# The 32 late modulation tiles: one-column matmuls replaced by streams past a 32-column stationary block

## What is computed

```
mod = silu(c) @ mod_w + mod_b          # (1024) @ (1024, 6*1024), six vectors of 1024
h   = rms_norm(x) * (1 + scale1) + shift1        # vectors 0, 1
x   = x + gate1 * norm(gla_mixer(h, h_ctx))      # vector 2
h   = rms_norm(x) * (1 + scale2) + shift2        # vectors 3, 4
x   = x + gate2 * norm(swiglu(h))                # vector 5
```

## Time and profile before

| | |
|---|---|
| median of 3 runs | 1826.99 us |
| lowest, highest | 1826.46, 1835.96 us |
| span of the profiled execution | 1833.4 us |
| PE busy in it | 1770.2 us, 97% |
| PEld, DVE, ACT, POOL busy | 1468.8, 813.0, 492.5, 111.6 us |
| mean granted PE clock | 0.951 of full |

### The profile page before, as it was taken

How to read it: one execution, slowest core, us unless ns; L and a number is a source line. 1 busy time by engine, 2 the same in 40 slices (tenths; PEclk the granted TensorE clock), 3 DMA queues, 4 the chain that set the end, 5 groups by cost and what they waited for, 6 DMA issues and landing times.

```text
span 1833.4 us, 20676 instructions
## 1 busy us (share of the span) xinstructions
PE 1770.2 (97%) x8502; PEld 1468.8 (80%) x8502; DVE 813.0 (44%) x955; ACT 492.5 (27%) x508; POOL 111.6 (6%) x95
## 2 busy tenths in 40 slices
PE   8999999999889999999899999999999999999997
PEld 3889987877768888888688888887897788888885
DVE  3654123444453343343444444344545544444444
ACT  3385123112232222222322222223132222222221
POOL 0000000000200000000200000111600400000000
PEclk9999997677889999999799999999999999999998
DMA  9132232001312222233132222333221222222231
GB/s 367 58 127 70 92 141 90 0 1 46 103 57 105 92 92 96 76 96 101 47 112 92 95 111 71 95 94 141 97 88 46 85 98 93 92 92 91 83 100 72
DMA packets 29288, 169.68 MB, mean 93 GB/s; under 512 B 3376, under 2 KB 3760, under 8 KB 15536
## 3 DMA queue, kind: packets, MB, share of 16 engines
q1 hardware_dynamic: 29232, 168.88, 26.4%
HBM read 166.77 MB, written 2.10 MB: 92 GB/s over the span
## 4 chain that ended last, share of the span: by engine, by line
PE 75%; issue 20%; DVE 2%; ACT 2%; POOL 1%; DMA 0%; POOLq 0%; DVEq 0%; SPq 0%; ACTq 0%
PE bank L476 75%; POOL qd L415 1%; ACT w_hi L989 0%; POOL root L386 0%; PE bank L687 0%; DMA mod_w<-in_mod 0%; DVE y_ffn L1875 0%; DVE w_lo L1322 0%; DVE tmp L1330 0%; DVE a_lo L1596 0%; ACT L1057 0%; ACT tmp L1061 0%; DVE y_gla L1585 0%; ACT tmp L1053 0%; ACT tmp L1057 0%
## 5 line engine op out<-in xcount | busy, mean ns | idle before, releaser
L476 PE MATMUL bank<-a_hi,w_hi 128*128 128x512 f32 x1376 | 545.3, 396 | 14.4 <-DVE a_lo L1596 8.4
L476 PE MATMUL bank<-a_hi,w_lo 128*128 128x512 f32 x1376 | 539.6, 392 | 0.0
L476 PE MATMUL bank<-a_lo,w_hi 128*128 128x512 f32 x1376 | 539.4, 392 | 0.0
L1322 DVE TENSOR_TENSOR w_lo<-w_raw,w_hi 128x2048 fp32r<-128x2048 f32 x144 | 333.8, 2318 | 428.9 <-ACT w_hi L989 428.4
L989 ACT ACTIVATE w_hi<-w_raw 128x2048 fp32r<-128x2048 f32 x144 | 275.5, 1913 | 622.5 <-PE bank L476 620.2
L476 PEld LDWEIGHTS bank<-a_hi,w_hi 128*128 128x128 f32 x1376 | 260.9, 190 | 73.2 <-issue 19.4
L476 PEld LDWEIGHTS bank<-a_hi,w_lo 128*128 128x128 f32 x1376 | 260.5, 189 | 55.5
L476 PEld LDWEIGHTS bank<-a_lo,w_hi 128*128 128x128 f32 x1376 | 260.8, 190 | 54.6 <-issue 1.2
L476 PE MATMUL bank<-g_hi,w_hi 128*128 128x512 f32 x528 | 205.4, 389 | 0.0
L476 PE MATMUL bank<-g_lo,w_hi 128*128 128x512 f32 x528 | 205.4, 389 | 0.0
L476 PE MATMUL bank<-g_hi,w_lo 128*128 128x512 f32 x528 | 205.4, 389 | 0.0
(11 more groups left out here) (238 smaller groups left out, 1650.9 us busy)
## 6 DMA issues: line engine op xcount, KB each, us to landing
w_raw<-in_ffn_in SPq DMA_DIRECT2D x66, 1024.0 KB, 4.8
w_raw<-in_ffn_out SPq DMA_DIRECT2D x24, 768.0 KB, 4.2
mod_raw<-in_mod SPq DMA_DIRECT2D x32, 512.0 KB, 3.6
w_raw<-in_ffn_out SPq DMA_DIRECT2D x24, 640.0 KB, 3.9
w_raw<-in_gla_in SPq DMA_DIRECT2D x12, 1024.0 KB, 5.8
w_raw<-in_mix_in SPq DMA_DIRECT2D x10, 1024.0 KB, 4.7
mod_w<-in_mod SPq DMA_DIRECT2D x8, 1024.0 KB, 15.3
w_raw<-in_gla_out SPq DMA_DIRECT2D x4, 1024.0 KB, 5.7
```

The costliest lines, as they stand in the source:

```text
L476: return pe.matmul(out, lhs, rhs, start=first, stop=last, skip_group_check=True)
L1322: V.tensor_tensor(flat(w_lo[s]), flat(w_raw[s]), flat(w_hi[s]).bitcast(F32), ALU.subtract).then_inc(lo_done[s], 1)
```

## The change

Four tiles are taken together, as group g of 0 to 7. Silu(c) becomes the stationary operand: `sc_wide` holds, for each of the 8 chunks of channels, a block of 32 columns of which the first is silu(c) and the others are zero. The weights of four tiles stream past it as 512 columns. Chunk k and chunk k+4 write to partitions 32(k mod 4) to 32(k mod 4)+31 of bank 7, so the results are four partial rows in one bank (`mod_lines`, 8 matmuls). ACT copies the bank to `mod_line`, and four matmuls against a column of ones sum the rows and turn them into four columns in bank 7 (`mod_columns_of`). DVE adds the bias (`mod_add`). All three engines use bank 7 in turn, so `mod_lines(g)` waits for `mod_add(g-1)`.

Groups 0 to 3 stand at the end of `v_unit` 0 to 3, groups 4 to 7 at the end of the four r units; the columns of a group stand one unit later than its lines. Nothing of the late tiles is left in units 0 to 3 or behind the scan. The weights come in 16 loads of 1 MB of 8 KB a partition into two buffers that lie in x's own 16 KB, and x is loaded a second time (2 MB) when they are done. The pieces below are, in order, the new functions on PE, the end of a v unit, the r units, ACT's copy, DVE in the v and in the r units, and SP.

```diff
-            def mod_tile(j):
-
-                pe.wait_ge(mod_loaded, cnt.next(mod_loaded, 16))
-                for k in range(KD):
-                    m = mm(bank[7][:, j:j + 1], mod_raw[:, k], sc[:, k, 0:1], k == 0, k == KD - 1)
-                m.then_inc(mod_used, 1)
+            def mod_lines(g):
+
+                if g == 0:
+                    pe.wait_ge(wide_done, 2)
+                else:
+                    pe.wait_ge(mod_added, g)
+                for half in range(2):
+                    pe.wait_ge(mod_loaded[half], cnt.next(mod_loaded[half], 16))
+                    for k in range(KD // 2):
+                        m = mm(bank[7][32 * k:32 * k + 32, :], sc_wide[:, half * (KD // 2) + k],
+                               mod_raw[half][:, :, k], half == 0, half == 1)
+                    m.then_inc(mod_used, 1)
+
+            def mod_columns_of(g):
+
+                pe.wait_ge(line_copied, g + 1)
+                for j in range(4):
+                    m = mm(bank[7][:, j:j + 1], mod_line[:, j * P:(j + 1) * P], ones[:, 0:1], True, True)
+                m.then_inc(mod_mapped, 1)
...
-                mod_tile(9 + 2 * h)
+                if h:
+                    mod_columns_of(h - 1)
+                mod_lines(h)
...
             for n in range(4):
-                unit(n % 2, ((0, 1), (3, 4))[n % 2], (a_hi, a_lo), tile=16 + 2 * n)
-                mod_tile(17 + 2 * n)
-            filled[7] = True
+                unit(n % 2, ((0, 1), (3, 4))[n % 2], (a_hi, a_lo))
+                mod_columns_of(3 + n)
+                mod_lines(4 + n)
+            mod_columns_of(7)
...
+            def line_copy(g):
+                act.wait_ge(mod_used, 2 * g + 2)
+                nc.scalar.activation(mod_line[:], bank[7][:], ACT.Copy).then_inc(line_copied, 1)
...
                 split_lo(h % 2)
+                if h:
+                    mod_add(h - 1)
...
             for n in range(4):
                 split_lo(n % 2)
-
-            dve.wait_ge(mod_used, cnt.next(mod_used, 3 * KD))
-            V.tensor_tensor(mod[:, 2 * KD:5 * KD, 0], bank[7][:, 0:3 * KD], col("mod_b", 2 * KD, 3 * KD), ALU.add).then_inc(free[7], 1)
+                mod_add(3 + n)
+            mod_add(7)
...
+            sp.wait_ge(mod_used, MOD_PARTS)
+            sp.dma_start(xT[:], a["x_fm"]).then_inc(x_again, 16)
```

More of the change, by code:

```diff
@@ L60 @@
 FIRST_MODS = 4
+MOD_PARTS = 16
 LAG = 2
@@ L142, in build @@
         mod_at = top[0]
-        mod_raw = place("mod_raw", [P, KD, P])
+        mod_line = place("mod_line", [P, T])
+        sc_wide = place("sc_wide", [P, KD, 32])
+        top[0] += KB
+        x_at = top[0]
         xT = place("xT", [P, KD, T])
+        mod_raw = [place(f"mod_raw{s}", [P, 4, KD // 2, P], F32, x_at + 8 * KB * s) for s in range(2)]
         act_at = here(32 * KB)
@@ L237, in build @@
         cols_ready = sem("modulation_columns_ready")
-        mod_loaded, mod_used = sem("mod_tile_loaded"), sem("mod_tile_used")
+        mod_loaded, mod_used = [sem(f"mod_part_loaded{s}") for s in range(2)], sem("mod_part_used")
+        mod_lined, line_copied = sem("mod_line_ready"), sem("mod_line_copied")
+        mod_mapped, mod_added, wide_done = sem("mod_columns_ready"), sem("mod_columns_added"), sem("wide_condition_done")
+        x_again = sem("x_loaded_again")
         cols_loaded, x_loaded, c_loaded = sem("cols_loaded"), sem("x_loaded"), sem("context_loaded")
@@ L315, in load, with load_parts @@
                 sp.dma_start(flat(w_raw[s])[:, 0:width], src).then_inc(raw_loaded[s], 16)
[L317 to L321, removed]
+            def load_parts(q0, q1):
+                for q in range(q0, min(q1, MOD_PARTS)):
+                    g, half = q // 2, q % 2
+                    if q >= 2:
+                        sp.wait_ge(mod_used, q - 1)
+                    w = KD // 2 * P
+                    sp.dma_start(mod_raw[half][:].rearrange("p j k o -> p j (k o)"),
+                                 a["mod25"][4 * g:4 * g + 4, :, half * w:(half + 1) * w].rearrange("j p w -> p j w")).then_inc(mod_loaded[half], 16)
             for n in range(8):
@@ L332, in _, with ffn @@
             sp.dma_start(reset[:], a["reset"]).then_inc(masks_loaded, 16)
-            load_tile(0)
-            for n in range(12):
+            for n in range(4):
+                load(n % 2, a["gla_in"][n + 2])
+            load_parts(0, 2)
+            for n in range(4, 12):
                 m = n + 2
                 load(m % 2, a["gla_in"][m] if m < 12 else a["gla_out"][m - 12])
-                load_tile(2 * n + 1)
-                load_tile(2 * n + 2)
+                load_parts(2 * n - 6, 2 * n - 4)
+            sp.wait_ge(mod_used, MOD_PARTS)
+            sp.dma_start(xT[:], a["x_fm"]).then_inc(x_again, 16)
             for m in (14, 15):
                 load(m % 2, a["gla_out"][m - 12])
-            load_tile(25)
-            def ffn(w_in, w_out, tiles=()):
+            def ffn(w_in, w_out):
                 both = {x[s]: 1 for x in (hi_done, lo_done) for s in range(2)}
@@ L358, in ffn @@
                         load(j % 2, src, (k1 - k0) * UC)
-            ffn(a["ffn0_in"], a["ffn0_out"], range(26, 32))
+            ffn(a["ffn0_in"], a["ffn0_out"])
             ffn(a["ffn1_in"], a["ffn1_out"])
@@ L485, in weights, with unit @@
                 return w_hi[s][:, k, c * P:(c + 1) * P], w_lo[s][:, k, c * P:(c + 1) * P]
-            def mod_tile(j):
-                pe.wait_ge(mod_loaded, cnt.next(mod_loaded, 16))
-                for k in range(KD):
-                    m = mm(bank[7][:, j:j + 1], mod_raw[:, k], sc[:, k, 0:1], k == 0, k == KD - 1)
-                m.then_inc(mod_used, 1)
-            def unit(s, banks, acts, by_chunk=None, says=None, tile=None, roots_to=None, streamed=False):
+            def mod_lines(g):
[14 more added lines that the diff above has]
+                m.then_inc(mod_mapped, 1)
+            def unit(s, banks, acts, by_chunk=None, says=None, roots_to=None, streamed=False):
                 pe.wait_ge(lo_done[s], cnt.next(lo_done[s]))
@@ L589, in gla_unit @@
                 s = n % 2
-                unit(s, banks, (a_hi, a_lo), norm_lo if n == 0 else None, tile=2 * n)
+                unit(s, banks, (a_hi, a_lo), norm_lo if n == 0 else None)
                 if n == 0:
@@ L720, in scan @@
                     take(6)
-                    take(7)
-                    filled[6] = filled[7] = False
+                    pe.wait_ge(mod_added, MOD_PARTS // 2)
+                    filled[6] = False
                 kv(0)
@@ L759, in _ @@
             for n in range(4):
-                unit(n % 2, ((0, 1), (2, 3))[n % 2], (a_hi, a_lo), norm_lo if n == 0 else None,
-                     tile=24 + n if n else None)
+                unit(n % 2, ((0, 1), (2, 3))[n % 2], (a_hi, a_lo), norm_lo if n == 0 else None)
             def double_norm():
@@ L800, in group @@
                         pe.wait_ge(up_free, cnt.now(up_free))
-                    unit(1, (2, 3), (a_hi, a_lo), None, up_ready, roots_to=5 if first and scaled else None,
-                         tile=31 if tiles else None)
+                    unit(1, (2, 3), (a_hi, a_lo), None, up_ready, roots_to=5 if first and scaled else None)
                     cnt.expect(up_free, CPU)
@@ L1322, in split_lo, with mod_add @@
                 V.tensor_tensor(flat(w_lo[s]), flat(w_raw[s]), flat(w_hi[s]).bitcast(F32), ALU.subtract).then_inc(lo_done[s], 1)
+            def mod_add(g):
+                dve.wait_ge(mod_mapped, g + 1)
+                V.tensor_tensor(mod[:, 2 * KD + 4 * g:2 * KD + 4 * g + 4, 0], bank[7][:, 0:4], col("mod_b", 2 * KD + 4 * g, 4),
+                                ALU.add).then_inc(mod_added, 1)
             def mean_square(b, n, width):
@@ L1360, in norm_parts @@
                 lower(KD - 1)
+            V.memset(flat(sc_wide), 0.0).then_inc(wide_done, 1)
+            dve.wait_ge(wide_done, 1)
+            dve.wait_ge(silu_c_done, 1)
+            V.tensor_copy(sc_wide[:, :, 0], sc[:, :, 0]).then_inc(wide_done, 1)
             V.memset(power[:], -0.5).then_inc(const_set, 1)
@@ L1510, in _ @@
                 split_lo(n % 2)
-            dve.wait_ge(mod_used, cnt.next(mod_used, 3 * KD))
-            V.tensor_tensor(mod[:, 2 * KD:5 * KD, 0], bank[7][:, 0:3 * KD], col("mod_b", 2 * KD, 3 * KD), ALU.add).then_inc(free[7], 1)
-            cnt.expect(free[7])
-            dve.wait_ge(free[7], cnt.now(free[7]))
+                mod_add(3 + n)
+            mod_add(7)
+            dve.wait_ge(mod_added, MOD_PARTS // 2)
             V.tensor_tensor(gain[:, 2], mod[:, 2 * KD:3 * KD, 0], col("norm_g", KD, KD), ALU.mult)
+            V.tensor_tensor(gain[:, 4], mod[:, 5 * KD:, 0], col("norm_g", 3 * KD, KD), ALU.mult)
             V.scalar_tensor_tensor(gain[:, 3], mod[:, 4 * KD:5 * KD, 0], 1.0, col("norm_g", 2 * KD, KD), ALU.add, ALU.mult).then_inc(dve_step, 1)
@@ L1696, in ffn @@
                 group(0, True)
[L1697 to L1703, removed]
                 for j in range(2):
```

18 lines of the change are left out of this document (4 added, 14 removed).

## The result

| | median, us | lowest to highest | runs | profiled execution: span, mean granted clock |
|---|---|---|---|---|
| before | 1829.91 | 1826.46 to 1835.96 | 4 | 1833.4, 0.951 |
| changed | 1859.16 | 1855.94 to 1859.96 | 4 | 1858.0 (of 1859.8 us), 0.938 |

The changed kernel takes 1.0148 times as long, with a 95% interval of 1.0124 to 1.0172. It is slower by 29 us, where 26.7 were forecast.

A forecast was written before the change was run, and what follows sets the result against it. PE, busy 97% of the span, was taken as the bound. Added 52.1 us (lines 15.6, last columns 1.6, pauses 34.9) less gains of 42.6, plus 17.2 for lower clock, made +26.7 on 1826.99: 1853.7 us, range 1833 to 1884.

The forecast's parts named there:

- units 0 to 3: Removing tiles 0 to 7 there gains 6.5 us instead of 13.6, as ACT's gate chain then becomes the bound.
- v and r units, and the scan's start: Added lines, last columns, pauses and lower clock, less 27.2 us for 16 tiles and 2.1 us for a wait.
- behind it: Behind the scan, removing tiles 25, 26, 27 and 31 gains 6.8 us; tiles 24, 28, 29 and 30 count nothing.
- The gain of the tiles: Late tiles taken off PE: 6.5 us in units 0 to 3, 27.2 in v and r units, 6.8 for four others.
- The lines: Four column strips overlap fully on PE: 1.95 us a group of 8 matmuls, 15.6 us for eight groups.
- The pauses: PE waits at unit ends for the add behind DVE's split: 3 x 4.7 + 4 x 5.2 = 34.9 us, seven columns included.
- The clock: PE's granted clock falls to half after all seven pauses, costing 17.2 us; bounds 0 and 22 us.
- wait for DVE's add: At the scan's start PE's wait for the one bias add, queued behind the last split, goes: 2.1 us gained.
- `ke_tok` release the first product: At the scan's start ACT's `ke_tok`, not the bias add, would be the last thing PE's first product waits for.
- The rival that came true by an edit: Each pause costs only columns, add and hand-overs, 1.4 us, and the clock holds: 1811 us; chance 0.07.
- the break-even: Pause length, with the clock up, below which the change wins: 3.6 us for each of the seven pauses.

The follow-up runs named there:

- e5: Kernel before, with nine late tiles (3 to 7, 24, 28, 29, 30) cut to one of eight matmuls each, loads kept: 1832.77 us, 1.0009 of before.
- e1: Changed kernel with DVE's bias add queued ahead of the split of the weights' lower part, in v and r units: 1814.96 us, 0.9903 of before.
- e6: Changed kernel with columns in mid-unit, add ahead of the split, and all lines in one strip of 32 partitions: 1860.06 us, 1.0152 of before.
- e8: Changed kernel with columns mid-unit, add before split, lines one unit early, last weight split behind the scan's first steps: 1813.19 us, 0.9896 of before.

## Why the prediction was right, point by point

| part | forecast, us | measured |
|---|---|---|
| units 0 to 3 | -6.5 | -6.6 |
| v and r units, and the scan's start | +40.0 | +36.7 |
| scan | 0 | -4.5 |
| behind it | -6.8 | -0.9 |
| sum | +26.7 | +24.6 in the spans; +29.2 in the medians |

(The forecast of the second row is 15.6 + 1.6 + 34.9 + 17.2 - 27.2 - 2.1.)

*Spans and medians.* The profiled execution of before lies 3.5 us above the median of before, that of the changed kernel 1.2 us under its own, so the spans differ by less. Most of it can be put down to the scan, which the change doesn't touch. The same code took 127.2 us there (granted clock 0.677), 122.1 in e5 (0.710), and 119.2 to 125.9 in the changed kernel and its variants, so the -4.5 of the scan is clock and no gain.

*The gain of the tiles.* Right in units 0 to 3, where ACT's chain took over as the bound, and shown by e5. The 27.2 us of the v and r units were not measured alone; they fit. e1's stage is 6.1 us shorter than before. My terms with the measured sizes (lines 8 x 1.86, columns to lines 7 x 1.21) give -27.2 - 2.1 + 14.9 + 1.6 + 8.5 = -4.3, and before had 5.2 us at half clock in that stage where e1 had 2.5, which is worth 1.3 more.

*The lines.* 1.95 us forecast, 1.85 measured at full clock. The four strips run side by side, as I had inferred from the row halves of the earlier trace rows; this was a guess from another direction of the array, and e6 made it a measurement. The estimate of 2.2 us that I had worked out from the Trainium skill's factor for four row strips (TensorE: Matmul & The Clock Gate, Part 3) was too much.

*The pauses.* 34.9 us forecast; 3 x 4.56 + 5.11 + 3 x 5.04 = 33.9 measured, from the columns' start to the lines'. The cause is shown by e1.

*The clock.* All seven pauses were followed by half clock, and 16.3 us of the 17.2 forecast came of it. It ran on through the last columns and the scores at the scan's start, which I had not forecast; there the wait for DVE's add that I had counted as a gain of 2.1 us was traded for a copy and columns at half clock. Nor did `ke_tok` release the first product, as I had expected: PE came to it without a wait.

*Behind the scan.* The profile gives back 0.9 us and not 6.8, but the term itself was there. Counted from the norm sums, the changed kernel was 5.9 us ahead of before at the end of the output units (tiles 25 to 27) and 8.0 us ahead once tile 31 was passed. Then 7.2 us came back in code that the change doesn't touch, most of it (1.8 and 4.1) in two places where it had more of the half clock. These are the two places in the trace of before, in the changed kernel's, and the first of them in e1's:

```profile
856.86:905.23 48.37, 39.83 (x164) 32.10 (x162) 22.45 (x25) 12.67 (x14) 12.34 (x9) 0.79 0.18 66
1380.74:1430.58 49.84, 45.99 (x250) 38.07 (x249) 25.11 (x39) 11.68 (x15) 11.78 (x7) 1.00 0.12 43
874.42:924.57 50.15, 41.59 (x163) 33.57 (x162) 22.44 (x25) 12.67 (x14) 12.32 (x9) 0.76 0.18 64
1401.33:1455.30 53.97, 50.37 (x250) 42.02 (x249) 25.11 (x39) 11.67 (x15) 11.76 (x7) 0.91 0.11 40
835.35:880.44 45.09, 36.54 (x164) 29.48 (x162) 23.01 (x25) 12.68 (x14) 12.29 (x9) 0.85 0.20 71
```

In the nine profiled executions of the changed code and its variants this part took either 1409.6 to 1409.9 us or 1414.4 to 1415.1, nothing between, and the first of the two places makes the difference: 50.15 us at a clock of 0.76 in the changed kernel, 45.09 at 0.85 in e1. At the second all nine, and e5 too, ran at 0.91, and only the execution of before at 1.00. So e5, the kernel before with nine tiles cut (four of them here, which the forecast counts at nothing), is the better base for this row: it took 1416.3 us with the clock of e1 at both places, and e1 took 6.6 us less, against the 6.8 forecast. What selects the clock there wasn't found.

*The rival that came true by an edit.* The forecast priced a pause of the add alone at 1811 us. e1 is that kernel, at 1815. So the break-even that it gave, 3.6 us a pause, was of use: with 1.2 us the change gains 1%, with 4.6 to 5.1 us it loses 1.5%.

## What to carry to other kernels

A step of 0.15 us on an idle engine costs what is queued ahead of it, here 4 us, and as the array waited for it, the half clock behind it cost some 0.6 of that again (16.3 us against 26.5). The Trainium skill (PSUM — Partial Sum Buffer, "Engine vs sequencer instructions") calls the queues of ACT, DVE and POOL strict FIFO. The trace agrees: the add, whose columns were done by 245, ran at 248.94, right behind the split that was queued ahead of it. So before a small round trip is put between an array and itself, write down what each helper has queued at that moment, and put the small step ahead of the long one that isn't urgent. Work moved off a busy engine is worth only what the next chain leaves: seven eighths of five tiles, 7.4 us, gave 1.6 us (e5), and the 2.5 us won ahead of the scan in e8 ended in a wait for an exponential of ACT.

## What was not expected of the hardware

Filling a wait with products that nobody reads made the kernel 22 us faster (1859.2 to 1837.4); 16.3 us of it are the half clock of the v and r units, the rest lies outside that stage. Four strips of 32 array columns, each fed by all 128 partitions, ran sixteen float32 passes of 512 columns in 1.86 us at full clock, 3.75 times as fast as one strip. And the same instructions behind the scan took one of two times, 1409.7 or 1414.9 us, by how long one stretch of half clock lasted.
